# Last output projection started ahead of the last head's attention, with the attention's gated outputs transposed head by head

## The chip, the cores and the metric

One core of a Trainium2 chip runs the whole kernel. The time is the device time of one execution in microseconds, and the number compared is the median of several executions. Lower is better. TensorE (PE) has two clock levels, 2.4 and 1.2 GHz; the profile gives the granted clock as a share of the full one. The other engines here are VectorE (DVE), ScalarE (ACT) and SyncE (SP, whose queue issues the loads); GpSimd (POOL) only fills constants at the start.

## What is computed

A two-layer backbone over 256 latent tokens and 256 context tokens, width 2048. Layer 0 is gated linear attention, layer 1 differential softmax attention with 8 heads. Only the latent tokens leave layer 1. Cut to layer 1 and its end:

```python
q, k, v, g = split(h @ diff_w_in, 4)          # h: normed, modulated; 2048 -> 4 x 2048
q, k = rope(rmsnorm(q)), rope(rmsnorm(k))     # 8 heads x 2 maps x 128
p = softmax(q @ k.T * 128 ** -0.5)            # per head and map, over latent and context keys
a = p[map 0] - lam * p[map 1]
o = a @ v                                     # 8 heads x 256
o = rmsnorm(o, subln_w) * (1 - lambda_init) * silu(g)
x = x + gate[:, None] * (o @ diff_w_out)      # 2048 -> 2048
```

## The kernel before

All arithmetic is fp32. A projection is made of chunks of 512 output columns. Each takes 16 k-tiles of 128, handled as 8 pairs. To reach fp32 accuracy with fast matmuls, weights and activations are each split in a high part and a rest: three matmuls (high x low, high x high, low x high) per k-tile and tile of 128 tokens. So a pair of k-tiles costs 12 matmuls of 128x512 for the 256 latent tokens, 24 for all 512.

The weights go through a ring of four slots (`w_raw`, `w_hi`, `w_lo`). SP loads a pair's raw weights (L317) once the slot's earlier `w_raw` is split; ACT makes the high part (`split`, L433) once PE has done the pair that used the slot; DVE makes the low part (`low`, L1059); PE multiplies (`project_pair`, L749). The functions `splits` and `lows` do several pairs. Each engine works strictly in the order in which its program is written, so the order of these calls among other work is the schedule. Chunks are numbered through the kernel: layer 1 has chunks 16 to 31, two a head (keys and values, chunk c, all four token tiles; queries and gates, chunk c+1, two tiles), and the output projection 32 to 35 (OUT1 = 32).

The attention of head h-1 runs on PE between the pairs of head h's first chunk: key transposes (L986), query transposes (L993), scores (L1002, fp32), weight transposes (L1011), values (L1018, fp32). Its DVE half is `attend`: copies out of PSUM, maxima (L1499), normalised weights (L1510, L1512), copies, then the copy of the output (L1523), its squares, inverse root and gated product (L1529) into `u1`, which is a part of the big tile `u`. `keys(h)` copies chunk c's banks (L1443) and norms and rotates the keys; `queries(h)` does the same for chunk c+1 (L1469). ACT has the exponentials (L643), the SiLU of the gates with its table load (L668), and logs and exponentials for inverse roots.

Head 7 has no next head. Its attention runs alone behind chunk 31. Then four gate rows are made: DVE writes a diagonal matrix of 512 gate values (`diagonal`, L1350), PE multiplies it by ones (`gate_rows`, L960), DVE copies the broadcast row out (L1357). Then the output projection starts: `transposing(3, u1, 2)` transposes the gated output k-tile by k-tile (L777) ahead of each pair of chunk 32, DVE multiplies by the norm weight (L1143) and takes the low part (L1158), ACT takes the high part (L461). Each of the four chunks runs through all 16 k-tiles into banks 0 and 1; `result(j)` on DVE multiplies by the gate row (L1559), which frees the bank, adds the residual (L1562), and ACT issues the store (L693).

Of the kernel before, what the change touches and what calls it, by code (L numbers as in the profile page):

```python
# [73 lines left out]
ADA_USES = 7  # L74

# [20 lines left out]
def build(nc, io, out):  # L96
    with ExitStack() as ctx:
# [99 lines left out]
        u1 = u[:, 2:4, :]  # L197
# [62 lines left out]
        pv_ok = sem("pv_ok")  # L260
        lam_t, lam_pr_ok, lam_e, lam_ok = sem("lam_t"), sem("lam_pr_ok"), sem("lam_e"), sem("lam_ok")
        y_ok = sem("y_ok")
        y_out = sem("y_out")
# [9 lines left out]
        def _(sp):  # L273
# [133 lines left out]
            attention_head(A_HEADS - 1, one_range(w1, 0))  # L407
            for j in range(0, 3):
                load_chunk(j + OUT1, one_range(w1, j * CW), one_range(w1, (j + 1) * CW))
            load_chunk(CHUNKS - 1, one_range(w1, 3 * CW), None)  # L410
# [12 lines left out]
        def _(act):  # L423
# [215 lines left out]
            def softmax(h):  # L639

                for i in range(4):
                    act.wait_ge(max_ok, h * 4 + (i + 1))
                    act.activation(probs[:, i // 2, i % 2], bank[4 + i][:], ACT.Exp, bias=smx[:, 0, i:i + 1],  # L643
                                   scale=A_D ** -0.5, accum_out=smx[:, 1, i:i + 1]).then_inc(p_ok, 1)

            BATCH = G_HEADS + 2

            def attention_head(h, before):
# [13 lines left out]
                splits(c + 2, range(0, 2))  # L662
                if h % 2 == 0:
                    modulation_rows(STARTUP + 2 * G_HEADS + 4 + h // 2)
                splits(c + 2, range(2, 4))
# [19 lines left out]
            softmax(A_HEADS - 1)  # L685
            rsqrt(A_HEADS * 3 + BATCH, 2)
            high_parts(3, hfu, OUT1)

            def store(j):

                act.wait_ge(y_ok, j * 2 + 2)
                for t in range(2):
                    act.dma_start(out[0][t * P:(t + 1) * P, bass.ds(j * CW, CW)], yrow[:, t]).then_inc(y_out, 16)  # L693

            for j in range(1, 4):
                splits(j + OUT1, range(4))
                store(j - 1)
                splits(j + OUT1, range(4, 8))
            store(3)
            act.wait_ge(y_out, 4 * 2 * 16)  # L700
# [3 lines left out]
        def _(pe):  # L704
# [250 lines left out]
            def gate_rows(first, batches):  # L955
                for n in range(first, first + batches):
                    pe.wait_ge(diag_ok, n + 1)
                    if n >= first + 2:
                        pe.wait_ge(gate_ok, n - 1)
                    pe.matmul(bank[5 + n % 2][:], ones[:], diag4[n % 2].rearrange("p a b -> p (a b)"),  # L960
                              start=True, stop=True).then_inc(gate_t, 1)

# [19 lines left out]
            def key_transposes(h):  # L982
                pe.wait_ge(k_ok, h + 1)
                for m in range(2):
# [36 lines left out]

            def attention_head(h, before=None, behind=None):
# [4 lines left out]
                project(c + 1, frees(h, 1), True, tiles=2)  # L1027
# [6 lines left out]
            for step in (key_transposes, query_transposes, attention_scores, weight_transposes, attention_outputs):  # L1034
                step(A_HEADS - 1)
            pe.wait_ge(u_ok, NT * G_HEADS + 2 * A_HEADS)
            gate_rows(8, 4)
            pe.wait_ge(gate_ok, 12)

            project(OUT1, lambda t: OUT1, True, tiles=2, before=transposing(3, u1, 2))  # L1040
            for c in range(OUT1 + 1, CHUNKS):
                project(c, lambda t: c, True, tiles=2)
# [3 lines left out]
        def _(dve):  # L1046
# [391 lines left out]

            def keys(h):
                c = h * 2 + DIFF  # L1440
                for t in range(NT):
# [18 lines left out]

            def queries(h):
                c = h * 2 + (DIFF + 1)
                lows(c + 1, range(0, 2))
# [18 lines left out]
            def attend(h):  # L1482

                c = h * 2 + (DIFF + 2)
                if c < OUT1:
                    low(c, 4)
# [4 lines left out]
                if c < OUT1:  # L1491
                    low(c, 5)
                dve.wait_ge(qt_t, h + 1)
                dve.tensor_copy(qT.rearrange("p m n -> p (m n)"), bank[6][:]).then_inc(qT_ok, 1)
                if c < OUT1:
                    low(c, 6)
# [6 lines left out]
                for t in range(2):  # L1503
                    s0, s1 = smx[:, 2, 2 * t:2 * t + 1], smx[:, 2, 2 * t + 1:2 * t + 2]
                    dve.wait_ge(p_ok, h * 4 + (2 * t + 2))
                    st.step(dve.reciprocal(smx[:, 2, 2 * t:2 * t + 2], smx[:, 1, 2 * t:2 * t + 2]))
                    st.wait()
                    st.step(dve.tensor_tensor(s1, s1, lam[:, 3:4], ALU.mult))
                    st.wait()
                    st.step(dve.tensor_scalar(probs[:, t, 1], probs[:, t, 1], s1, None, ALU.mult))  # L1510
                    st.wait()
                    dve.scalar_tensor_tensor(probs[:, t, 0], probs[:, t, 0], s0, probs[:, t, 1], ALU.mult,  # L1512
                                             ALU.subtract).then_inc(a_ok, 1)
                if c < OUT1:
                    low(c, 7)
                    lows(c + 1, range(0, 2))
# [3 lines left out]
                if c < OUT1:  # L1520
                    low(c + 1, 2)
# [28 lines left out]
            def result(j, first):  # L1550
# [13 lines left out]
                if j < 3:  # L1564
                    low(j + OUT1 + 1, 3)
# [48 lines left out]
```

## Time and profile before

| | us |
|---|---|
| median of 3 runs | 1812.04 (1810.16 to 1813.54) |
| profiled execution, its own time | 1809.72 |
| its span, first to last instruction | 1807.9 |
| mean granted clock of TensorE | 0.975 |
| PE, DVE, ACT busy | 1702.6, 908.8, 557.0 |

In the rows of a time line the columns are start and duration in us, engine, line, operation, output and inputs, shapes and how many instructions were merged, and in brackets the idle time ahead of it with the instruction that ended it. A matmul's duration is modelled and longer than its distance to the next one: matmuls recorded at 0.39 us follow each other every 0.227 us.

### The profile page before, as it was taken

To read this page: it belongs to the slowest core of one execution; us is meant where nothing else is said; L and a number is where in the kernel's file an instruction comes from. 1 tells how busy PE (TensorE), PEld (TensorE's weight loads), DVE (VectorE), ACT (ScalarE), POOL (GpSimd) and SP (SyncE) were. 2 spreads that over 40 slices of the span, in tenths; PEclk is the share of its full clock that TensorE was granted. 3 is DMA by queue.
4 is the path that set the end of the run, shared out by engine and by line. 5 is a ranking of instruction groups with operands and counts; after the bars stand their busy time and mean duration, and the time that the engine had idled before them with its cause. 6 is when DMAs were issued, how large, how long until landed. Compare 5 with 4: busy or idle time off the path is not lost.

```text
span 1807.9 us, 19679 instructions
## 1 busy us (share of the span) xinstructions
PE 1702.6 (94%) x8012; PEld 1280.8 (71%) x8012; DVE 908.8 (50%) x1534; ACT 557.0 (31%) x813; POOL 2.2 (0%) x9
## 2 busy tenths in 40 slices
PE   4888999999999999989999799999999999998698
PEld 1455786678678777857777587877787787776476
DVE  2326443545264425536333557575564756557564
ACT  3213332333233313333222323242332323233232
POOL 0000000000000000000000000000000000000000
PEclk9889999999999999989999899999999999999899
DMA  8993434442443255225555326244433524423063
GB/s 314 320 332 116 164 102 153 167 163 84 140 163 106 71 175 173 72 70 164 174 191 182 105 77 232 83 139 147 147 126 117 188 80 131 160 94 121 20 197 118
DMA packets 181502, 265.54 MB, mean 147 GB/s; under 512 B 11978, under 2 KB 95876, under 8 KB 180868
## 3 DMA queue, kind: packets, MB, share of 16 engines
q1 hardware_dynamic: 175680, 256.16, 42.9%
q10 hardware_dynamic: 5732, 8.13, 1.5%
q8 instruction: 63, 1.03, 0.2%
q14 instruction: 27, 0.22, 0.0%
HBM read 262.14 MB, written 2.10 MB: 146 GB/s over the span
## 4 chain that ended last, share of the span: by engine, by line
PE 88%; DVE 7%; ACT 2%; DMA 2%; issue 1%; ACTq 1%; SPq 0%; DVEq 0%
PE bank L749 70%; PE bank L716 5%; PE bank L931 2%; PE bank L880 2%; PE bank L1018 2%; PE bank L1002 2%; PE bank L724 1%; DVE w_lo L1059 1%; DVE work L1135 1%; PE bank L876 1%; PE bank L777 1%; ACT w_hi L433 1%; DMA sel_sb<-in_sel 1%; DVE work L1379 1%; DVE u L1382 0%
## 5 line engine op out<-in xcount | busy, mean ns | idle before, releaser
L749 PE MATMUL bank<-w_lo,acts_hi 128*128 128x512 f32 x1664 | 669.1, 402 | 14.9 <-DVE acts_lo L1158 7.1
L749 PE MATMUL bank<-w_hi,acts_lo 128*128 128x512 f32 x1664 | 651.1, 391 | 0.0
L749 PE MATMUL bank<-w_hi,acts_hi 128*128 128x512 f32 x1664 | 651.0, 391 | 0.0
L1059 DVE TENSOR_TENSOR w_lo<-w_raw,w_hi 128x1024 fp32r<-128x1024 f32 x288 | 351.2, 1222 | 489.9 <-ACT w_hi L433 489.6
L433 ACT ACTIVATE w_hi<-w_raw 128x1024 fp32r<-128x1024 f32 x288 | 303.6, 1057 | 880.0 <-PE bank L749 866.9
L749 PEld LDWEIGHTS bank<-w_lo,acts_hi 128*128 128x128 f32 x1664 | 314.1, 189 | 129.9 <-issue 39.7
L749 PEld LDWEIGHTS bank<-w_hi,acts_lo 128*128 128x128 f32 x1664 | 313.8, 189 | 67.2
L749 PEld LDWEIGHTS bank<-w_hi,acts_hi 128*128 128x128 f32 x1664 | 314.5, 189 | 62.4 <-issue 1.7
L749 PE MATMUL bank<-acts_hi,w_lo 128*128 128x512 f32 x256 | 107.6, 420 | 15.6 <-DVE acts_lo L1180 15.6
L749 PE MATMUL bank<-acts_hi,w_hi 128*128 128x512 f32 x256 | 103.4, 404 | 0.0
L749 PE MATMUL bank<-acts_lo,w_hi 128*128 128x512 f32 x256 | 103.1, 403 | 0.0
L716 PE MATMUL bank<-ada_w,silu_p 128*32 128x512 f32 x624 | 86.8, 632 | 4.3 <-DMA ada_w<-in_ada_w 4.3
L749 PEld LDWEIGHTS bank<-acts_hi,w_lo 128*128 128x128 f32 x256 | 50.3, 196 | 43.3 <-DVE acts_lo L1180 19.2
L1114 DVE TENSOR_TENSOR mod<-bank,cols 128x8 f32<-128x8 f32 x24 | 3.9, 163 | 112.1 <-PE bank L724 112.1
L749 PEld LDWEIGHTS bank<-acts_lo,w_hi 128*128 128x128 f32 x256 | 50.2, 196 | 11.4
L749 PEld LDWEIGHTS bank<-acts_hi,w_hi 128*128 128x128 f32 x256 | 50.3, 197 | 10.7 <-issue 0.7
L931 PE MATMUL bank<-work 128*128 128x512 f32 x96 | 42.0, 593 | 0.0
L880 PEld LDWEIGHTS bank<-work 128*64 128x64 f32 (+1 forms) x512 | 37.8, 150 | 4.9
L880 PE MATMUL bank<-work 128*64 128x64 f32 (+2 forms) x512 | 40.7, 256 | 0.0
L461 ACT ACTIVATE acts_hi<-work 128x512 fp32r<-128x512 f32 (+1 forms) x48 | 25.6, 553 | 43.6 <-DVE work L1143 30.8
L1158 DVE TENSOR_TENSOR acts_lo<-work,acts_hi 128x512 fp32r<-128x512 f32 (+1 forms) x48 | 28.6, 595 | 18.5 <-ACT acts_hi L461 18.2
L716 PEld LDWEIGHTS bank<-ada_w,silu_p 128*32 128x32 f32 x624 | 12.9, 110 | 33.6 <-issue 25.2
(163 smaller groups left out, 1185.1 us busy)
## 6 DMA issues: line engine op xcount, KB each, us to landing
ada_w<-in_ada_w SPq DMA_DIRECT2D x78, 1024.0 KB, 7.6
w_raw<-in_diff_w_in SPq DMA_DIRECT2D x256, 256.0 KB, 3.0
w_raw<-in_gla_w_in SPq DMA_DIRECT2D x192, 256.0 KB, 3.1
u<-in_ada_w SPq DMA_DIRECT2D x16, 1024.0 KB, 9.2
w_raw<-in_gla_w_out SPq DMA_DIRECT2D x64, 256.0 KB, 3.5
w_raw<-in_diff_w_out SPq DMA_DIRECT2D x64, 256.0 KB, 3.6
u<-in_x SPq DMA_DIRECT2D x2, 1024.0 KB, 6.1
u<-in_ctx SPq DMA_DIRECT2D x2, 1024.0 KB, 10.7
```

The lines of the kernel that those rows point to most:

```text
L433: act.activation(w_hi[:, p % RING], raw[:, p % RING], ACT.Copy).then_inc(w_hi_ok, 1)
L461: act.activation(hi[:, k, 0:n * P], src[:, k % 2, 0:n * P], ACT.Copy).then_inc(hi_ok, 1)
L716: last = pe.matmul(b[32 * j:32 * j + 32, :], silu_p[:, 4 * q + j, :], quad_slot[slot][:, j, :], start=(q == 0), stop=(q == 3), skip_group_ ...
L724: last = pe.matmul(b[:, 2 * n:2 * n + 2], ada_rows[:, n * P:(n + 1) * P], sel[:], start=(n == 0), stop=True, skip_group_check=True)
L749: last = pe.matmul(bank[t][:], a, b, start=(k == 0 and i == 0), stop=(k == NK - 1 and i == 2))
L777: last = pe.transpose(bank[4 + k % 3][:, t * P:(t + 1) * P], src[:, t, k * P:(k + 1) * P], ident[:])
L880: return pe.matmul(out_, k_part, q_part, start=start, stop=True, skip_group_check=True)
L931: last = pe.matmul(bank[4 + t % 3][:], at[:, b, col:col + P], v_sb[:, kt, :], start=(i == 0), stop=(i == len(READ[t]) - 1))
L1002: pe.matmul(bank[4 + i][:], qT[:, m, t * P:(t + 1) * P], kT[:, m, :], start=True, stop=True)\
L1018: last = pe.matmul(bank[6][:, t * A_DV:(t + 1) * A_DV], aT[:, kt, t * P:(t + 1) * P], kv[:, kt, A_DV:CW], start=(kt == 0), stop=(kt == NT ...
L1059: dve.tensor_tensor(w_lo[:, p % RING], raw[:, p % RING], w_hi[:, p % RING].bitcast(F32), ALU.subtract)\
L1158: dve.tensor_tensor(lo[:, k, 0:width], buf[:, k % 2, 0:width], hi[:, k, 0:width].bitcast(F32), ALU.subtract).then_inc(acts_ok, 1)
```

## The change

The gated output of each head is kept where the attention output was (`o1`), and PE transposes it in the next head's second chunk, behind its pair 1, into bank 5. DVE multiplies it by the norm weight into `uT1`, a full transposed tile in the place of `u1`. In head 7's second chunk PE also makes the four gate rows, and DVE their diagonals and copies, in the two parts of `ada_w`. ACT and DVE make the high and low parts of k-tiles 0 to 13 behind the splits of the first output pairs.

The output projection becomes 32 output pairs in a new order: chunk 0's pairs 0 to 6, chunk 1's pairs 0 to 6, then pair 7 of chunk 0 and of chunk 1, then chunks 2 and 3 as before. Chunks 0 and 2 use banks 0 and 1, chunks 1 and 3 banks 2 and 3. Head 7's attention steps stand behind output pairs 1, 3, 4, 9, 10 and 13. The loads follow the new order; stores 0 and 1 are issued one behind the other.

```diff
+def out1_pair(s):
+    if s < 14:
+        return s // 7, s % 7
+    if s < 16:
+        return s - 14, 7
+    return s // 8, s % 8
+OUT1_DONE = (15, 16, 24, 32)
...
-        u1 = u[:, 2:4, :]
+        uT1 = u[:, 2:4, :].rearrange("p t (k n) -> p (t k) n", n=2 * P)
+        gate1 = ada_w[:, 0].rearrange("p j n -> p (j n)")
+        diag1 = [ada_w[:, 1, i].rearrange("p (a b) -> p a b", b=P) for i in range(2)]
...
# ACT
+            def high_out1(p):
+                for k in (2 * p, 2 * p + 1):
+                    if p < 7:
+                        act.wait_ge(u1T_ok, p + 1)
+                        act.wait_ge(pair_done, (OUT1 - 1) * PAIRS + (p + 1 + RING))
+                    else:
+                        act.wait_ge(u1T_ok, A_HEADS)
+                    act.activation(hi[:, k, 0:2 * P], uT1[:, k], ACT.Copy).then_inc(hi_ok, 1)
...
+                if h == A_HEADS - 1:
+                    for p in range(4):
+                        split(c + 2, p)
+                        high_out1(p)
...
-            softmax(A_HEADS - 1)
+            for p in range(4, 7):
+                split(OUT1, p)
+                high_out1(p)
+            splits(OUT1, range(7, 8))
+            splits(OUT1 + 1, range(0, 1))
+            softmax(A_HEADS - 1, range(0, 2))
+            splits(OUT1 + 1, range(1, 2))
+            softmax(A_HEADS - 1, range(2, 4))
+            splits(OUT1 + 1, range(2, 7))
             rsqrt(A_HEADS * 3 + BATCH, 2)
-            high_parts(3, hfu, OUT1)
+            high_out1(7)
+            splits(OUT1 + 1, range(7, 8))
...
+            splits(OUT1 + 2, range(4))
+            store(0)
+            store(1)
+            splits(OUT1 + 2, range(4, 8))
...
# PE
+            def output_transposes(h):
+                pe.wait_ge(u_ok, NT * G_HEADS + 2 * h + 2)
+                for j in range(2):
+                    for t in range(2):
+                        last = pe.transpose(bank[5][:, (2 * j + t) * P:(2 * j + t + 1) * P],
+                                            o1[:, t, j * P:(j + 1) * P], ident[:])
+                last.then_inc(ut_t, 1)
...
+                def second(p):
+                    if h > 0 and p == 1:
+                        output_transposes(h - 1)
+                    if h == A_HEADS - 1 and p in (1, 2, 6, 7):
+                        gate_rows({1: 8, 2: 9, 6: 10, 7: 11}[p])
+                project(c + 1, frees(h, 1), True, tiles=2, after=second)
...
+            def output_pair(s):
+                j, kp = out1_pair(s)
+                c, p = OUT1 + s // PAIRS, s % PAIRS
+                pe.wait_ge(w_split, c * PAIRS + (p + 1 + RING))
+                for e in range(2):
+                    k, wh, wl = 2 * kp + e, w_hi[:, p % RING, e], w_lo[:, p % RING, e]
+                    if j < 2:
+                        pe.wait_ge(acts_ok, 3 * NK + k + 1 if j == 0 else 4 * NK if kp == 7 else 3 * NK + 14)
+                    for t in range(2):
+                        b = 2 * (j % 2) + t
...
+            behind_last = {1: key_transposes, 3: query_transposes_last, 4: attention_scores, 9: weight_transposes,
+                           10: attention_outputs, 13: output_transposes}
+            for s in range(4 * PAIRS):
+                output_pair(s)
+                if s in behind_last:
+                    behind_last[s](A_HEADS - 1)
...
# DVE, keys(7) and queries(h)
+                if h == A_HEADS - 1:
+                    dve.wait_ge(ada_taken, STARTUP + BACKGROUND)
+                    for i in range(2):
+                        gate_diagonal(8 + i, i)
...
+                if h > 0:
+                    outputs_out(h - 1)
+                if h == A_HEADS - 1:
+                    for i in range(2):
+                        gate_out(8 + i, i)
+                        gate_diagonal(10 + i, i + 2)
+                    for p in range(2):
+                        low(c + 1, p)
+                        low_out1(p)
...
+                if h == A_HEADS - 1:
+                    low_out1(2)
+                    gate_out(10, 2)
...
# DVE, behind queries(7)
+            gate_out(11, 3)
+            low_out1(3)
+            low(OUT1, 4)
+            low_out1(4)
+            keys_out(last_head)
+            low(OUT1, 5)
+            low_out1(5)
+            low(OUT1, 6)
+            low_out1(6)
+            queries_out(last_head)
+            low(OUT1, 7)
+            low(OUT1 + 1, 0)
+            maxima(last_head)
+            low(OUT1 + 1, 1)
+            weights(last_head, 0)
+            low(OUT1 + 1, 2)
+            weights(last_head, 1)
+            lows(OUT1 + 1, range(3, 5))
+            weights_out(last_head)
+            low(OUT1 + 1, 5)
+            gated(last_head)
+            low(OUT1 + 1, 6)
+            outputs_out(last_head)
+            low_out1(7)
+            low(OUT1 + 1, 7)
...
+            lows(OUT1 + 2, range(0, 3))
+            result(0)
+            low(OUT1 + 2, 3)
+            result(1)
+            lows(OUT1 + 2, range(4, 8))
+            lows(OUT1 + 3, range(0, 3))
+            result(2)
+            lows(OUT1 + 3, range(3, 8))
+            result(3)
```

`gate_diagonal` and `gate_out` are one DVE product of 128x512 and one DVE copy of 128x512; `outputs_out` is two DVE products of 128x256 out of bank 5; `low_out1(p)` two DVE subtractions of 128x256. `keys_out`, `queries_out`, `maxima`, `weights`, `weights_out` and `gated` are the parts of the former `attend`, unchanged but for where `gated` writes.

## Rows read from the trace of the kernel before

**Rows 1.** The page: engines' busy time, the w_lo group, the weight loads.

```profile
PE 1702.6 (94%) x8012; PEld 1280.8 (71%) x8012; DVE 908.8 (50%) x1534; ACT 557.0 (31%) x813; POOL 2.2 (0%) x9
L1059 DVE TENSOR_TENSOR w_lo<-w_raw,w_hi 128x1024 fp32r<-128x1024 f32 x288 | 351.2, 1222 | 489.9 <-ACT w_hi L433 489.6
w_raw<-in_diff_w_out SPq DMA_DIRECT2D x64, 256.0 KB, 3.6
```

**Rows 2.** Busy time by stretch: length, PE, PEld, DVE, ACT, POOL, clock, DMA share, GB/s.

```profile
1639.30:1661.20 21.90, 21.90 (x97) 18.09 (x97) 18.04 (x26) 8.69 (x10) 0.00 (x0) 1.00 0.50 161
1661.20:1706.20 45.00, 22.42 (x61) 12.18 (x60) 27.74 (x60) 9.34 (x19) 0.00 (x0) 0.73 0.08 27
1706.20:1733.00 26.80, 26.04 (x120) 20.41 (x121) 19.79 (x36) 12.26 (x22) 0.00 (x0) 1.00 0.32 105
1733.00:1756.10 23.10, 22.35 (x97) 17.89 (x97) 12.32 (x13) 8.51 (x9) 0.00 (x0) 1.00 0.70 219
```

**Rows 3.** The chain of waits, last head's attention: start us, us, what.

```profile
1672.92 3.64 PE bank L1002 x4
...
1684.52 6.38 PE bank L1018 x16
```

**Rows 4.** Time line of PE beside projections: transposes, scores, values.

```profile
1598.42 0.60 PE L993 MATMUL bank<-ident_sb,work 128*128 128x128 f32 x4
1598.77 0.48 PE L749 MATMUL bank<-w_lo,acts_hi 128*128 128x512 f32 x1
...
1604.33 3.59 PE L1002 MATMUL bank<-work 128*128 128x512 f32 x8
...
1630.43 3.61 PE L1018 MATMUL bank<-work 128*128 128x256 f32 x16
```

**Rows 5.** Time line: the copies ahead of chunk 31, its first matmul, two diagonals.

```profile
1638.52 2.48 DVE L1443 COPY work<-bank 128x512 f32<-128x512 f32 x4
1639.35 0.47 PE L749 MATMUL bank<-w_lo,acts_hi 128*128 128x512 f32 x1
...
1695.47 1.29 DVE L1350 TENSOR_TENSOR work<-ident_sb,mod 128x512 f32<-128x512 f32 x2
```

**Rows 6.** Time line of DVE: w_lo in a queue, the last head's query chain.

```profile
1651.62 2.35 DVE L1059 TENSOR_TENSOR w_lo<-w_raw,w_hi 128x1024 fp32r<-128x1024 f32 x2
1653.89 0.68 DVE L1427 TENSOR_TENSOR work<-work 128x512 f32<-128x512 f32 x1
...
1661.01 1.28 DVE L1469 COPY work<-bank 128x512 f32<-128x512 f32 x2
...
1670.29 0.68 DVE L1427 TENSOR_TENSOR work<-work 128x512 f32<-128x512 f32 x1
```

**Rows 7.** Time line: from a transposed tile to its high and low part.

```profile
1703.83 0.88 DVE L1143 TENSOR_SCALAR work<-bank,cols 128x256 f32<-128x256 f32 x2 [0.53 <-PE bank L777]
1704.35 0.81 ACT L461 ACTIVATE acts_hi<-work 128x256 fp32r<-128x256 f32 x2 [10.61 <-DVE work L1143]
...
1704.80 0.42 DVE L1158 TENSOR_TENSOR acts_lo<-work,acts_hi 128x256 fp32r<-128x256 f32 x1
```

**Rows 8.** Time line of PE: first matmuls of a later output chunk, the very last.

```profile
1756.08 0.47 PE L749 MATMUL bank<-w_lo,acts_hi 128*128 128x512 f32 x1 [0.44 <-DVE work L1559]
...
1757.31 0.51 PE L749 MATMUL bank<-w_lo,acts_hi 128*128 128x512 f32 x1 [0.30 <-DVE work L1559]
...
1801.56 0.39 PE L749 MATMUL bank<-w_hi,acts_lo 128*128 128x512 f32 x1
```

**Rows 9.** A matmul after a short wait; a stretch (columns as in rows 2).

```profile
1092.52 0.47 PE L749 MATMUL bank<-w_lo,acts_hi 128*128 128x512 f32 x1 [1.78 <-DVE work L1443]
...
1692.00:1694.00 2.00, 0.00 (x0) 0.00 (x0) 1.39 (x5) 0.41 (x2) 0.00 (x0) 0.83 0.00 0
```

**Rows 10.** Time line of PE: the first pair of chunk 12, layer 0's output projection.

```profile
803.72 0.80 PE L749 MATMUL bank<-w_lo,acts_hi 128*128 128x512 f32 x1 [2.78 <-DVE acts_lo L1158]
...
809.01 0.52 PE L749 MATMUL bank<-w_lo,acts_hi 128*128 128x512 f32 x1
```

More of the change, by code:

```diff
@@ L637, in _, with softmax @@
             high_parts(2, hf, DIFF)
-            def softmax(h):
-                for i in range(4):
+            def softmax(h, parts=range(4)):
+                for i in parts:
                     act.wait_ge(max_ok, h * 4 + (i + 1))
@@ L952, in _ @@
                 gla_head(h)
[L955 to L961, printed above, removed]
             def block_gates(j):
@@ L1020, in attention_outputs, with gate_rows @@
                 last.then_inc(pv_ok, 1)
+            def output_transposes(h):
[5 more added lines that the diff above has]
+                last.then_inc(ut_t, 1)
+            def gate_rows(n):
+                pe.wait_ge(diag_ok, n + 1)
+                if n >= 10:
+                    pe.wait_ge(gate_ok, n - 1)
+                pe.matmul(bank[6 + n % 2][:], ones[:], diag1[n % 2].rearrange("p a b -> p (a b)"),
+                          start=True, stop=True).then_inc(gate_t, 1)
             def attention_head(h, before=None, behind=None):
@@ L1033, in _, with query_transposes_last @@
                                           5: weight_transposes, 6: attention_outputs})
[L1034 to L1042, printed above, removed]
+            def query_transposes_last(h):
+                pe.wait_ge(gate_ok, 12)
+                query_transposes(h)
+            def output_pair(s):
[8 more added lines that the diff above has]
+                        b = 2 * (j % 2) + t
+                        if k == 0:
+                            pe.wait_ge(freed[b], (OUT1 if b < 2 else DIFF + A_HEADS) + j // 2)
+                        x = slice(t * P, (t + 1) * P)
+                        for i, (a, w) in enumerate(((hi[:, k, x], wl), (hi[:, k, x], wh), (lo[:, k, x], wh))):
+                            last = pe.matmul(bank[b][:], a, w, start=(k == 0 and i == 0), stop=(k == NK - 1 and i == 2))
+                        if k == NK - 1 and t == 0:
+                            last.then_inc(acc_ok, 1)
+                last.then_inc(pair_done, 1)
+            behind_last = {1: key_transposes, 3: query_transposes_last, 4: attention_scores, 9: weight_transposes,
[4 more added lines that the diff above has]
+                    behind_last[s](A_HEADS - 1)
         @block.vector
@@ L1519, in attend, with gated @@
                     dve.tensor_copy(flat(aT[:, 2 * b:2 * b + 2]), bank[4 + b][:]).then_inc(aT_ok, 1)
-                if c < OUT1:
-                    low(c + 1, 2)
+            def gated(h):
                 dve.wait_ge(pv_ok, h + 1)
@@ L1528, in attend @@
                 for t in range(2):
-                    dve.scalar_tensor_tensor(u1[:, t, bass.ds(h * A_DV, A_DV)], o1[:, t], stat[:, 2, t:t + 1],
-                                             silu_ag[:, t], ALU.mult, ALU.mult).then_inc(u_ok, 1)
+                    dve.scalar_tensor_tensor(o1[:, t], o1[:, t], stat[:, 2, t:t + 1], silu_ag[:, t], ALU.mult, ALU.mult)\
+                        .then_inc(u_ok, 1)
+            def attend(h):
+                c = h * 2 + (DIFF + 2)
+                low(c, 4)
+                keys_out(h)
+                low(c, 5)
+                queries_out(h)
+                low(c, 6)
+                maxima(h)
+                for t in range(2):
+                    weights(h, t)
+                low(c, 7)
+                lows(c + 1, range(0, 2))
+                weights_out(h)
+                low(c + 1, 2)
+                gated(h)
             lows(DIFF + 1, range(0, 3))
@@ L1567, in _ @@
-            result(0, True)
-            for j in range(1, 4):
-                result(j, False)
+            last_head = A_HEADS - 1
+            gate_out(11, 3)
[12 more added lines that the diff above has]
+            low(OUT1 + 1, 1)
```

134 lines of the change are left out of this document (71 added, 63 removed).

## Prediction

> **What bounds the kernel now.** I read the page first: PE is busy 1702.6 of 1807.9 us [rows 1], so only time in which PE stands still, or runs at its lower clock, can be won. The table by stages says where that is [rows 2]. Projection chunk 31 (1639.3 to 1661.2) is PE from end to end at clock 1.00. Then come 45.0 us with 22.42 us of PE at a mean clock of 0.73: the last head's attention, four gate rows and the first transposes of the output, with no projection to fill the waits. The first output chunk takes 26.8 us (transposes and waits between its matmuls), the later ones about 23.1. The chain of waits inside the 45 us goes back and forth between DVE and PE, and PE's share runs at the low clock: the four scores matmuls are on it for 3.64 us though only part of them shows, and the 16 value matmuls for 6.38 us [rows 3], against 3.3 us for the same 16 beside the projections [rows 4]. So the end is set by PE's work after 1639.35 plus PE's waits, and the largest wait is the one gap.
>
> **The unit prices.** One pair of k-tiles with two token tiles is 12 matmuls; 96 matmuls of chunk 31 take 21.8 us, so a pair costs 2.72 us. Beside projections a group of 4 transposes costs 0.45 us (from 1598.42 to 1598.77 and 0.1 more before the next matmul runs evenly), 8 cost 0.9, the 4 scores matmuls 3.4 and the 16 value matmuls 3.4 (recorded at 3.59 and 3.61, which overlap their neighbours by 0.2) [rows 4]. A gate row is one fp32 matmul of 128x512 like a score: 0.9 us each with its switch. On DVE, two w_lo take 2.27 us (1651.62 to the next start at 1653.89), so 1.14 each when queued [rows 6]; a 128x512 copy or diagonal in a queue is 0.62 to 0.65 [rows 5, 6]; a low part of 128x256 is recorded at 0.42 [rows 7] and costs 0.35 to 0.4 in a queue.
>
> **PE's work after 1639.35, part by part.** The moved work isn't less, it only lies elsewhere. Chunk 31 and the 32 output pairs: 40 x 2.72 = 108.8. Beside them: two groups of output transposes (heads 6 and 7) 0.9, gate rows 3.6, key transposes 0.9, query transposes 0.45, scores 3.4, weight transposes 0.85, values 3.4: together 13.5. Heads 0 to 5 are transposed earlier, inside chunks that run without a gap, so 6 x 0.45 = 2.7 us are added there in full; the DVE copies behind them (2 x 0.4 us a head) fall into DVE's waits for ACT before its w_lo (489.9 us before 288 of them, 1.7 each [rows 1]), and cost nothing while these last. Sum without waits: 125.0. In the trace the same stretch lasts to 1801.56 + 0.23 = 1801.8 [rows 8], 162.4 us.
>
> **The waits that I expect, by walking the queues.** (a) Two gate diagonals stand on DVE ahead of the copies that free banks 0 and 1 for chunk 31. Today the copy starts at 1638.52 and PE at 1639.35, just when chunk 30 ends [rows 5], so there is no slack: 1.2 us. (b) After chunk 31 and gate row 11 (0.9) PE needs bank 0, which DVE copies only behind the low parts of output pairs 0 to 2 and one gate copy. DVE reaches it about 1.0 us after chunk 31's end, frees it at 1.7: 0.8 us. Two pairs, key transposes and a pair take PE to 10.8 us after chunk 31. (c) The queries' chain (copies to the rotated result, 1661.01 to 1670.97, so 8.7 us behind the copies' end [rows 6]) ends at 10.9; behind it the last gate copy (0.62) and a low part (0.4) let PE start pair 3 at about 11.9: 1.0 us. Pair 3, query transposes, pair 4 end near 17.8. (d) DVE has in its queue, before the copy of the transposed queries: 3 w_lo (3.4), 7 low parts (2.6), key copies (1.3), and that copy (0.65): 8.0 us from 11.9, so the scores start at 19.8: 2.0 us. (e) From there five pairs cover maxima and softmax: DVE needs 3.2 (maxima), 3.2 (weights) and four w_lo (4.6), with ACT waiting once for a pair; my walk has the weights ready 4 us before PE has done pair 9, the transposed weights 2 us before pair 10 ends, and the gated output 3.5 us before pair 13 ends. So none. (f) Behind the last output transposes there is nothing to fill: DVE's two copies, ACT's high part, DVE's low part, 1.9 us in all (0.48 + 0.4 + 0.45 + 0.42 and latencies, after 1703.83, 1704.35 and 1704.80 [rows 7]). (g) At the switch to the third chunk DVE has three w_lo ahead of the multiply that frees bank 0: 0.8, and 0.5 more for bank 1, much like today's 0.44 and 0.30 as shown plus gaps that the modelled ends hide, 1.1 in all [rows 8]. The third-to-fourth switch uses the other banks: none. Sum 1.2 + 0.8 + 1.0 + 2.0 + 1.9 + 1.3 = 8.2 us.
>
> The ring of four weight slots gives 8.2 us from the release of a slot to its use, against 1.22 us for DVE's part of a split and less for ACT's, and weight loads (3.6 us to landing [rows 1]) are asked for one ring turn ahead; SP's queue holds only those. The stores of result chunks 0 and 1 are issued on ACT one behind the other, ahead of the split of pair 4 of the third chunk; it waits to about 1732 and is used at 1737. ACT's high parts (2 x 0.41 a pair) fit in its waits. The tail behind PE's last matmul stays: two multiplies, two adds, the store.
>
> **The sum.** 125.0 + 8.2 + 0.2 for further switches = 133.4 us instead of 162.4: 29.0 less. The profiled execution took 1809.72 us at a span of 1807.9; the median of the runs is 1812.04. I take 29 us from the median: 1783.0 us.
>
> **Unknown costs and bounds.** No row shows a short copy behind transposes of head h-1 competing in chunk c+1; it lies between 0 (hidden, as the w_lo of [rows 6] are) and 7 x 0.8 = 5.6 us on PE; I take 0, as those waits are seen everywhere. Nor does one show output pairs with 6 waits in 55 us. If DVE is 20% quicker through the walk than I book it, the waits shrink by 2 to 3 us (no lower: PE's 125.0 are fixed). If it is 20% slower, (b), (c), (d) grow by about 4 us.
>
> **Weighed against the skill: the clock.** The trace shows what waits do to PE's clock. After 1.78 us of waiting the matmul at 1092.52 took 0.47 us, a full-speed one [rows 9]. Idle from 1690.9 on (the end of the value matmuls [rows 3]), the clock fell to its lower level some 2.4 us later: 0.83 over 1692 to 1694 is 1.00 for 1.3 us and 0.50 for the rest [rows 9]. At 803.72, after 2.78 us of waiting, twelve matmuls ran 5.3 us instead of 2.7 and only then came back to 2.4 GHz [rows 10]. My longest waits, (d) and (f), are 2.0 and 1.9, between these. The Trainium skill, "TensorE: Matmul & The Clock Gate", section "A second HAM failure mode: psum-queue depth-cycling", says that many short idles between matmul groups make the clock swing between its two levels; by that rule this order, with six short waits, could lose some of its gain. The trace agrees for idles of 2.4 us and more and not for 1.8.
>
> **Rivals.** (1) The clock falls to 1.2 GHz once or twice behind (d) or (f). For it: the 2.4 us row. Against it: the 1.78 us row, and the dense matmuls on both sides. Price 2.6 us each from [rows 10], up to 3.4 if it hits the scores or values (which double): 1786 to 1790. (2) DVE becomes the bound of the last head: from the last quarter of chunk 31 to the weights it hardly rests, and as its queue is strict, lateness shows in (b), (c), (d) and then in the ring. Twice the waits (b) to (f), 7 more: 1788 to 1794. Against it: PE's five pairs of cover. (3) The walk books too much waiting: 1777 to 1780. (4) Slower than before: the clock, once down in (c) or (d), doesn't come back through the mixed stretch of pairs, transposes and fp32 matmuls. PE work at 1.2 GHz takes twice its time, so 29 us of full-speed work must be run at the low level, that is 58 us of the time, before the change loses; the whole mixed stretch and a chunk at it: 1816. For it: the last head's 16 value matmuls took 6.38 us, low for their whole length [rows 3]; against it, one dense pair restored 2.4 GHz at 809 [rows 10]. (5) The change doesn't overlap as it says, PE in order waiting for the last head's chain ahead of the output pairs: about 1808. The walk finds PE's waits (the freed bank, one low part, the transposed queries) far short of that.
>
> **How the numbers follow.** Forecast 1783.0, own range 1780 to 1786: 60%. Rival 1: 18%. Rival 2: 11%. Rival 3: 6%. Rival 4: 2%. Rival 5: 3%. The range reaches from the edge of rival 3 over rival 1 and half of rival 2: 1779.5 to 1791. A measurement of this kernel tells about 0.2% (3.6 us) from no change; faster by more has all of 1, 2, 3 and the forecast and half of 5: 0.96; within 0.2%: 0.02; slower: 0.02.
>
> **What would show it.** The first output pair should start about 1.7 us after chunk 31's last matmul, and scores, value matmuls and both transposes stand between output pairs. Chunk 31 should start 1.2 us late behind a COPY at DVE. PE's waits in the stretch should sum to 8 us with the two longest before the scores and before the first k-tile of pair 7; clock 1.00 throughout; PE's last matmul 29 us earlier. Wrong would be: waits before w_split (the ring starved), a clock under 1.00 between chunk 31 and the end, or gaps in heads 1 to 6 beyond 0.45 us each.

## The result and the profile after

The changed kernel takes 1781.46 us (1781.14 to 1782.85), beside 1811.1 us for the one before in the same comparison: ratio 0.9838, interval 0.9821 to 0.9855, 29.6 us less. The forecast was 1783.0. The profiled execution took 1782.85 us at a span of 1780.9, 27.0 us under the span before. It is the slowest of its four; 1.6 us of it are a fall of the clock that is shown below. The same kernel was run and profiled once more later, 1782.86 us at a span of 1781.0 ("changed again" below).

Busy time by stretch in the changed kernel (columns as in [rows 2]):

```profile
1642.60:1664.50 21.90, 20.84 (x90) 16.46 (x90) 19.89 (x32) 8.84 (x13) 0.00 (x0) 1.00 0.37 120
1664.50:1687.70 23.20, 20.92 (x92) 15.70 (x90) 20.71 (x42) 13.96 (x22) 0.00 (x0) 1.00 0.41 134
1687.70:1723.00 35.30, 33.32 (x145) 26.37 (x146) 21.89 (x40) 10.94 (x19) 0.00 (x0) 1.00 0.42 136
...
1731.00:1774.70 43.70, 43.40 (x191) 35.40 (x189) 22.61 (x25) 12.82 (x13) 0.00 (x0) 1.00 0.53 159
```

The 45 us with half of PE idle at a mean clock of 0.73 [rows 2] are gone. From chunk 31 to the last output pair PE is busy for at least nine tenths of each stretch, and DVE for about as much of the first two.

Who PE waited for from 1640 to 1775, changed kernel (total us, times, longest):

```profile
PE bank L1121 <- DVE acts_lo L1578: 2.7, 2, 2.0
PE bank L1048 <- DVE work L1622: 1.2, 1, 1.2
PE bank L802 <- DVE work L1548: 1.1, 1, 1.1
PE bank L1121 <- DVE work L1720: 0.7, 2, 0.4
PE bank L1121 <- DVE work L1602: 0.3, 1, 0.3
```

L802 is the projection, L1121 the output pairs, L1048 the scores. These are the waits (a) L1548, (b) L1602, (c) and (f) L1578, (d) L1622 and (g) L1720 of the prediction, and no other. In this stretch PE did not wait for a split pair of weights (w_split). The idle shown is less than the loss, because a matmul's recorded end is modelled. By distance to the next start, less 0.23 us for a matmul that simply follows, they are:

| wait | booked | measured |
|---|---|---|
| (a) ahead of chunk 31 | 1.2 | 1.2 |
| (b) first output pair | 0.8 | 0.5 |
| (c) pair 3 | 1.0 | 0.9 |
| (d) scores | 2.0 | 1.4 |
| (f) behind the last output transposes | 1.9 | 2.1 |
| (g) switch to the third chunk | 1.3 | 1.1 |
| sum | 8.2 | 7.2 |

The time line of the changed kernel at some of these places, PE and DVE (columns as before):

```profile
1569.17 0.60 PE L1072 MATMUL bank<-ident_sb,work 128*128 128x128 f32 x4
1569.52 0.48 PE L802 MATMUL bank<-w_lo,acts_hi 128*128 128x512 f32 x1
...
1641.78 1.29 DVE L1532 TENSOR_TENSOR ada_w<-ident_sb,mod 128x512 f32<-128x512 f32 x2
1642.98 2.48 DVE L1548 COPY work<-bank 128x512 f32<-128x512 f32 x4
...
1686.98 0.68 DVE L1622 COPY work<-bank 128x512 f32<-128x512 f32 x1
...
1722.74 0.47 PE L1121 MATMUL bank<-w_lo,acts_hi 128*128 128x512 f32 x1 [1.97 <-DVE acts_lo L1578]
```

The first two rows answer [rows 4]: a head's output transposes take 0.35 us to the next matmul and nothing waits for them. The diagonals at 1641.78 push the bank copies behind the end of chunk 30 (1642.6); in [rows 5] the copies start before that end.

The one thing that the table of waits lacks is the clock. Changed kernel, profiled execution, then the later execution of the same kernel:

```profile
1721.00:1723.00 2.00, 0.26 (x1) 0.29 (x2) 1.45 (x4) 1.28 (x3) 0.00 (x0) 1.00 0.07 26
1723.00:1725.00 2.00, 2.00 (x7) 1.54 (x7) 1.58 (x2) 2.00 (x3) 0.00 (x0) 0.57 0.00 0
1725.00:1727.00 2.00, 2.00 (x7) 1.58 (x6) 1.92 (x2) 0.28 (x1) 0.00 (x0) 0.58 0.47 151
```

```profile
1722.00:1724.00 2.00, 0.40 (x4) 0.16 (x2) 1.08 (x3) 0.65 (x3) 0.00 (x0) 1.00 0.28 102
1724.00:1726.00 2.00, 1.63 (x7) 1.40 (x8) 1.51 (x3) 2.00 (x4) 0.00 (x0) 1.00 0.00 0
```

In the first, PE falls to 1.2 GHz behind wait (f) for about 3.4 us; the pair takes 4.4 us instead of 2.8. In the second the same wait of 1.97 us leaves the clock alone. This was expected of the second execution before it ran: the fall may stay away or move, and 1.6 us in this stretch would show it (191.2 against 189.6 us in the table below). As a whole it was no faster than the first, 1782.86 against 1782.85, because its clock fell earlier in the kernel, behind a wait near 1090 us.

### The profile page after: what moved, and what is told of

Its sections match the earlier page's. It is cut to its first block, busy times and chain, and to the rows that moved or that the text cites. A ratio compares the mean times of both kernels' runs of the same rounds, so it can differ in the third digit from the quotient of the medians.

```text
span 1780.9 us, 19693 instructions
## 1 busy us (share of the span) xinstructions
PE 1691.0 (95%) x8012; PEld 1276.5 (72%) x8012; DVE 906.5 (51%) x1534; ACT 555.5 (31%) x813; POOL 2.2 (0%) x9
## 4 chain that ended last, share of the span: by engine, by line
PE 88%; DVE 7%; DMA 2%; ACT 2%; issue 1%; ACTq 1%; SPq 0%; DVEq 0%
PE bank L802 67%; PE bank L769 5%; PE bank L1121 4%; PE bank L984 2%; PE bank L933 2%; PE bank L1048 2%; PE bank L1064 2%; PE bank L777 1%; DVE w_lo L1148 1%; DVE work L1224 1%; PE bank L929 1%; DMA sel_sb<-in_sel 1%; DVE work L1468 1%; PE bank L830 1%; DVE u L1471 1%
## 5 line engine op out<-in xcount | busy, mean ns | idle before, releaser
L802 PE MATMUL bank<-w_lo,acts_hi 128*128 128x512 f32 x1536 | 619.5, 403 | 13.3 <-DVE acts_lo L1247 6.1
L802 PE MATMUL bank<-w_hi,acts_lo 128*128 128x512 f32 x1536 | 600.8, 391 | 0.0
L802 PE MATMUL bank<-w_hi,acts_hi 128*128 128x512 f32 x1536 | 600.3, 391 | 0.0
L802 PEld LDWEIGHTS bank<-w_lo,acts_hi 128*128 128x128 f32 x1536 | 289.6, 189 | 121.2 <-issue 39.3
L802 PEld LDWEIGHTS bank<-w_hi,acts_lo 128*128 128x128 f32 x1536 | 289.5, 188 | 62.6
L802 PEld LDWEIGHTS bank<-w_hi,acts_hi 128*128 128x128 f32 x1536 | 290.2, 189 | 58.3 <-issue 2.4
L802 PE MATMUL bank<-acts_hi,w_lo 128*128 128x512 f32 x256 | 107.0, 418 | 15.6 <-DVE acts_lo L1269 15.6
L802 PE MATMUL bank<-acts_hi,w_hi 128*128 128x512 f32 x256 | 102.6, 401 | 0.0
L802 PE MATMUL bank<-acts_lo,w_hi 128*128 128x512 f32 x256 | 102.5, 400 | 0.0
L802 PEld LDWEIGHTS bank<-acts_hi,w_lo 128*128 128x128 f32 x256 | 49.9, 195 | 43.2 <-DVE acts_lo L1269 19.2
L802 PEld LDWEIGHTS bank<-acts_lo,w_hi 128*128 128x128 f32 x256 | 49.8, 195 | 11.2
L802 PEld LDWEIGHTS bank<-acts_hi,w_hi 128*128 128x128 f32 x256 | 50.1, 196 | 10.5 <-issue 0.7
L1121 PE MATMUL bank<-w_lo,acts_hi 128*128 128x512 f32 x128 | 51.9, 405 | 3.8 <-DVE acts_lo L1578 2.7
L1121 PE MATMUL bank<-w_hi,acts_lo 128*128 128x512 f32 x128 | 50.6, 396 | 0.0
L1121 PE MATMUL bank<-w_hi,acts_hi 128*128 128x512 f32 x128 | 50.4, 394 | 0.0
```

What stands on the lines that cost most here:

```text
L802: last = pe.matmul(bank[t][:], a, b, start=(k == 0 and i == 0), stop=(k == NK - 1 and i == 2))
L1121: last = pe.matmul(bank[b][:], a, w, start=(k == 0 and i == 0), stop=(k == NK - 1 and i == 2))
```

## The experiments

All experiments start from the changed kernel. Several effects are smaller than what executions of one kernel differ by ahead of the last head: the first matmul of chunk 30 came at 1589.73 in one and at 1591.36 in the other execution of the changed kernel. Those 1.6 us come from that earlier fall (rows in the last section). So beside the times I compare the stretch from that matmul to the end of the span ("last stretch"):

| kernel | time, us | last stretch, us |
|---|---|---|
| before | 1811.1 | 221.4 |
| changed | 1781.5 | 191.2 with the fall of the clock, 189.6 without (changed again) |
| alone | 1803.1 | 212.9 |
| alone_warm | 1799.8 | 207.9 |
| one_chunk | 1790.1 | 197.7 |
| scores_early | 1785.5 | 195.2 |
| diag_late | 1778.6 | 190.2 (with a fall) |
| out_early | 1780.5 | 187.4 |
| all_three | 1775.5 | 184.9 |
| five | 1772.0 | 182.1 |
| dve_keys2 | 1784.2 | 192.6 |
| dve_weights2 | 1781.2 | 191.1 (with a fall) |

Those of alone, alone_warm, one_chunk, all_three and five are medians of four; the rest of the experiments ran once each, so for them the last stretch carries the argument, and not the time.

**Is it the cover?** The last head's attention put back in front of the output pairs:

```diff
-            behind_last = {1: key_transposes, 3: query_transposes_last, 4: attention_scores, 9: weight_transposes,
-                           10: attention_outputs, 13: output_transposes}
+            behind_last = {}
+            for step in (key_transposes, query_transposes_last, attention_scores, weight_transposes,
+                         attention_outputs, output_transposes):
+                step(A_HEADS - 1)
```

with DVE's and ACT's parts of it ahead of the splits of pair 4 and later.

> The changed kernel, but the last head's attention and its output transposes stand ahead of all output pairs on PE, and its DVE and ACT parts ahead of the weights' splits from pair 4 on; transposing head by head, early gate rows, pair order and banks stay. Theory (the gain is the cover that output pairs give to the last head's attention): the attention's chain is bare again, PE's first output pair starts about 19 us later against the work left, 1800 us, and the clock falls again in the scores and value matmuls. Rival (the gain comes from early transposes, early gate rows and the banks; the order of attention and pairs matters little): below 1787 us.

It took 1803.1 us (0.9951 of before, 0.9935 to 0.9968). PE's four longest waits from 1640 us on:

```profile
PE bank L1034 <- DVE ada_w L1535: 9.1, 1, 9.1
PE bank L1067 <- DVE work L1654: 4.6, 1, 4.6
PE bank L1052 <- DVE work L1638: 4.1, 1, 4.1
PE bank L1043 <- DVE work L1619: 1.4, 1, 1.4
```

The last stretch is 23.3 us longer than the changed kernel's at full clock. So the cover is most of the gain; what is left of it, 7.8 us by the medians, is early transposes, early gate rows and the second pair of banks together, which no run separates. The forecast of 19 was 4 us short; how much low clock it held is not on record.

**What part of that is the clock?** The same kernel with PE kept at work in the waits:

```diff
+            def spin(n):
+                pe.wait_ge(freed[2], DIFF + A_HEADS)
+                for _ in range(n):
+                    pe.matmul(bank[2][:, 0:P], ones[:], ident[:], start=True, stop=True)
...
+            key_transposes(last_h)
+            spin(36)
+            query_transposes_last(last_h)
```

> As the previous kernel, with fp32 matmuls of 128x128 on constant tiles (into a bank that is overwritten later) put into PE's waits between the attention steps: 36, 4, 17, 4, 20 and 7 of them. Theory: what the overlap gains is mostly the waits themselves; keeping PE active keeps 2.4 GHz and gives back only the low-clock part, 1.9 us at the scores, 0.5 at the weight transposes and 3.0 at the values: about 5.5 us under the previous kernel, 1795. Rival (the low clock was the main loss of the gap): 10 us or more under it.

The clock stayed at 1.00 until the end of the work, and the last stretch is 4.9 us shorter (medians: 3.3), close to the 5.5 expected. The clock is worth more than that: the last group of fillers stands where alone has no wait. There the first output pair starts 0.76 us behind the start of the output transposes (1705.28 to 1706.04), and here 1.97 us (1699.62 to 1701.59). With these 1.2 us, about 6 of the 23.3 us that the cover is worth are clock and 17 are the waits themselves.

Time line of PE in alone, the weight transposes and the values, and then in alone_warm, the scores (as the values beside projections [rows 4], the scores are at full speed there; in alone the values run as long as in [rows 3]):

```profile
1692.08 1.10 PE L1052 MATMUL bank<-ident_sb,work 128*128 128x128 f32 x8 [4.12 <-DVE work L1638]
1694.12 6.55 PE L1059 MATMUL bank<-work 128*128 128x256 f32 x16 [0.94 <-DVE work L1644]
```

```profile
1680.93 3.70 PE L1043 MATMUL bank<-work 128*128 128x512 f32 x8 [0.92 <-DVE work L1634]
```

**Is one chunk enough cover?** Order by chunks, with the weight transposes behind pair 5, values and output transposes behind pair 6:

```diff
-    if s < 14:
-        return s // 7, s % 7
-    if s < 16:
-        return s - 14, 7
     return s // 8, s % 8
```

> The changed kernel with only chunk 0 of the output projection as cover: all 8 pairs of chunk 0, then chunk 1, and so on; weight transposes behind pair 5, values and output transposes behind pair 6; result 0 is taken early. Theory: 2 instead of 9 pairs lie between the scores and the output transposes, so PE waits 2.3 us for the weights, 4.5 for the gated output and 2.0 for its high and low parts, while the switch between chunks 1 and 2 no longer waits: about 5 to 7 us slower than the changed kernel, 1787. Rival (one chunk covers enough, the second chunk and its banks are not needed): within 1.5 us of the changed kernel.

1790.1 us (0.9882, 0.9867 to 0.9897), against 1787 expected, and 8.1 us more in the last stretch. PE's waits:

```profile
PE bank L1066 <- DVE work L1651: 4.6, 1, 4.6
PE bank L1115 <- DVE acts_lo L1572: 2.7, 2, 2.0
PE bank L1051 <- DVE work L1635: 2.1, 1, 2.1
PE bank L1042 <- DVE work L1616: 1.2, 1, 1.2
```

The wait for the gated output (4.6, L1651) and for the weights (2.1, L1635) are the two that I had worked out, and the switch (g) is gone as expected. The last 2 us or so, which the expectation did not have, are clock: it was low from 1710 to about 1717. So the second column chunk is worth 8 of the 29 us.

**The clock by itself.** Scores ahead of output pair 4 instead of behind it, which makes wait (d) 4.0 us:

```diff
-            behind_last = {1: key_transposes, 3: query_transposes_last, 4: attention_scores, 9: weight_transposes,
+            behind_last = {1: key_transposes, 3: lambda h: (query_transposes_last(h), attention_scores(h)), 9: weight_transposes,
```

> The changed kernel with the last head's scores right behind the query transposes, ahead of output pair 4. It doubles wait (d): PE idles 4.1 us instead of 1.4 ahead of the scores. Theory (clock): after so long an idle the scores start at or soon fall to 1.2 GHz; the wait costs 2.7 us, the clock 1.6 to 3.4 more: 1786 to 1788. Rival: the clock holds at 1.00 through the scores and only the 2.7 us show, 1784. Beside that, the weights come later, since maxima stand behind a split that waits for pair 4; four pairs of slack should hide it.

Time line of PE and busy time by stretch, same kernel:

```profile
1686.35 6.67 PE L1048 MATMUL bank<-work 128*128 128x512 f32 x8 [4.01 <-DVE work L1622]
```

```profile
1684.00:1686.00 2.00, 0.00 (x0) 0.00 (x0) 2.00 (x4) 0.00 (x0) 0.00 (x0) 0.88 0.62 189
1686.00:1688.00 2.00, 1.65 (x2) 0.84 (x3) 1.42 (x2) 0.00 (x0) 0.00 (x0) 0.50 0.85 278
```

The clock fell before the scores began and held low through all of them: 6.67 us instead of 3.7, so 3.0 us for the clock on top of 2.7 for the wait. The last stretch is 5.6 us longer than the changed kernel's at full clock, which is both; nothing else came of it. The time, 1785.5, lies just under the 1786 to 1788 expected. The wait of 1.97 us at (f) was there too, without a fall.

**The waits one by one.** Diagonals behind the copies of the keys:

```diff
-                if h == A_HEADS - 1:
-                    dve.wait_ge(ada_taken, STARTUP + BACKGROUND)
-                    for i in range(2):
-                        gate_diagonal(8 + i, i)
                 for t in range(NT):
                     complete(h * 4 + 3 * DIFF, c, t)
                     dve.tensor_copy(kv[:, t], bank[t][:]).then_inc(freed[t], 1)
+                if h == A_HEADS - 1:
+                    for i in range(2):
+                        gate_diagonal(8 + i, i)
```

(the wait stays where it was).

> The changed kernel with only the two gate diagonals moved behind the copies of the last head's keys. Theory: the 1.06 us wait of PE ahead of chunk 31 goes, and stays gone, since everything behind it moves with PE: last matmul 1.1 us earlier, about 1780.3. Rival (the next wait takes it up, because DVE reaches the query copies no earlier): wait (b) grows from 0.5 to 1.6 us and the time stays.

Wait (a) was gone and all the others kept their size (1.3 at the scores, 2.0 at (f), the clock falling behind it as in the changed kernel's profiled execution). The last stretch is 1.0 us shorter than that one's: of the 1.2 us measured at (a), 1.0 came back, and (b) did not take it up. The time, 1778.6, is 1.7 us under the 1780.3 expected; chunk 30 started at 1586.56 already, and that is not the edit's.

Output transposes one pair earlier:

```diff
-                           10: attention_outputs, 13: output_transposes}
+                           10: attention_outputs, 12: output_transposes}
```

> The changed kernel with only the last output transposes moved from behind pair 13 to behind pair 12. Theory: the gated output is ready at 1716.6, pair 12 ends at 1717.4, so PE does not wait for it; pair 13 covers the 1.9 us of copies and parts, so wait (f) goes, and with no idle PE the clock stays at 1.00 there: 2.0 + 1.6 = 3.6 us, 1777.9. Rival (the fall of the clock has nothing to do with that wait): the clock still falls near 1723, 2.0 us.

Wait (f) was gone, the clock stayed at 1.00 up to the tail. The last stretch is 2.2 us shorter than the changed kernel's at full clock and 3.8 shorter than that with the fall, against 2.0 and 3.6. The time, 1780.5, missed the 1777.9 expected: this execution had the fall behind the wait near 1090 us, as changed again had it.

These two with two more, the gate copy 10 behind the query copies and `queries_out` ahead of `low(OUT1, 6)`:

```diff
+            queries_out(last_head)
             low(OUT1, 6)
             low_out1(6)
-            queries_out(last_head)
```

> The changed kernel with its waits (a), (b), (d) and (f) attacked by order alone: the two gate diagonals behind the copies of the last head's keys, the third gate copy behind the query copies, the copy of the transposed queries one pair earlier on DVE, the output transposes behind pair 12 instead of 13. Theory (the remaining waits are set by what stands ahead in DVE's queue): 1.2 + 0.5 + 1.4 + 2.0 us of waits go, and with (f) the fall of the clock at 1723 that cost 1.6: 5 to 6.7 us faster, 1775 to 1776.5. Rival (the waits are in a chain, and one removed comes back at the next): 2 us or less.

1775.5 us (0.9801, 0.9785 to 0.9817), 6.3 us less in the last stretch than the profiled execution of the changed kernel and 4.7 less than the one at full clock. Of PE's waits only two lines are left:

```profile
PE bank L1121 <- DVE acts_lo L1579: 1.3, 1, 1.3
PE bank L1121 <- DVE work L1722: 0.7, 2, 0.4
```

The total lies in the expected 1775 to 1776.5. The first line is (c), which grew from 0.9 to 1.4 us by start distances: PE comes earlier, the queries' chain does not. So a part of what (b) gave, 0.5 us, moved on to the next wait, as the rival said; the rest stayed gained.

Wait (c) and (g) on top: the fourth gate copy and the low part of pair 3 in DVE's idle time ahead of the inverse roots, and result 0 behind two splits instead of three:

```diff
                 squares(q_t, q_raw, 4)
-                inverse_rms(h * 3 + (BATCH + 2), 4, A_D)
+                if h < A_HEADS - 1:
+                    inverse_rms(h * 3 + (BATCH + 2), 4, A_D)
+                else:
+                    dve.tensor_scalar(stat[:, 1, 0:4], stat[:, 0, 0:4], 1.0 / A_D, EPS, ALU.mult, ALU.add)\
+                        .then_inc(mean_ok, 1)
+                    gate_out(11, 3)
+                    low_out1(3)
+                    dve.wait_ge(rs_ok, h * 3 + (BATCH + 2))
+                    newton(4)
...
-            lows(OUT1 + 2, range(0, 3))
+            lows(OUT1 + 2, range(0, 2))
             result(0)
-            low(OUT1 + 2, 3)
+            lows(OUT1 + 2, range(2, 4))
             result(1)
```

> The kernel with the four order edits, and two more: in the last head's queries the fourth gate copy and the low part of output pair 3 stand in DVE's wait for the inverse roots (2.2 us idle), and result 0 is taken between the low parts of the third chunk's pairs 1 and 2 instead of behind three of them. Theory (waits are set by DVE's order): wait (c), 1.45 us in that kernel, and the two waits of (g), 1.06 us, go: 2.5 us less, 1773.0. Rival (by now PE's own work bounds, or the waits move on to the scores): 1 us or less.

1772.0 us (0.9776, 0.9759 to 0.9792), and another 2.8 us less in the last stretch, for 2.5 expected. PE has no wait left:

```profile
1641.00:1667.00 26.00, 26.00 (x110) 20.02 (x110) 25.07 (x42) 11.44 (x17) 0.00 (x0) 1.00 0.43 143
1667.00:1720.00 53.00, 53.00 (x240) 42.67 (x239) 42.33 (x77) 25.58 (x41) 0.00 (x0) 1.00 0.44 142
```

DVE's wait ahead of the inverse roots, 2.2 us in the changed kernel, now holds two pieces of work (time line of DVE):

```profile
1669.06 0.69 DVE L1538 COPY ada_w<-bank 128x512 f32<-128x512 f32 x1
1669.66 0.75 DVE L1579 TENSOR_TENSOR acts_lo<-u,acts_hi 128x256 fp32r<-128x256 f32 x2
1671.49 0.16 DVE L1158 TENSOR_TENSOR stat<-stat 128x4 f32<-128x4 f32 x1 [1.08 <-ACT stat L469]
```

**Where does DVE's lateness count?** Three copies in a row put into its queue at two places, all else as in the changed kernel:

```diff
+            for _ in range(3):
+                st.step(dve.tensor_copy(d2m[:], d1m[:]))
+                st.wait()
             keys_out(last_head)
```

> The changed kernel with three DVE copies of 128x512 between unused tiles, one waiting for the other (about 0.7 us each, 2.1 in all), ahead of the copies of the last head's transposed keys. Theory (DVE's queue sets wait (d)): PE's wait before the scores grows from 1.4 to 3.5 us and the rest follows, 2.1 us slower, and the longer idle makes the fall of the clock likely (1.6 to 3 us more). Rival (DVE has slack there): the wait stays at 1.4.

```profile
1682.17 1.34 DVE L1690 COPY d2m<-d1m 128x512 f32<-128x512 f32 x3
1683.54 1.29 DVE L1618 COPY work<-bank 128x512 f32<-128x512 f32 x2
```

The three copies took 1.37 us, not 2.1: I had priced a copy out of SBUF by the rows of copies out of PSUM. The wait at (d) grew from 1.4 to 2.8 us, by just that, and the clock fell in the scores, which were recorded at 5.4 us instead of 3.7. Last stretch 3.0 us longer.

The same ahead of `weights_out`:

> The same three DVE copies, but ahead of the copies of the last head's transposed weights. Theory (five pairs and more cover this part, the prediction booked 2 us of slack for the transposed weights): no new wait of PE before the value matmuls, time as the changed kernel within 0.5 us beside its clock. Rival (DVE is the bound of the whole last head): 2.1 us slower there too.

PE had no new wait; the last stretch equals that of the changed kernel with its fall of the clock (191.1 and 191.2), and a fall behind (f) was there as well.

## Why the prediction was right

The forecast of 1783.0 stands 1.5 us above the median, and the mechanism is the one that it walked through. By the traces the sum of 133.4 us fits within 0.1: 132.1 measured behind chunk 30, 3.0 for the transposes ahead of it, less 1.6 for the fall of the clock, are 133.5. That this is so close is partly luck, because three errors cancel: the waits were booked 1.0 too high, the switches 0.8 and the transposes 0.3 too low. And the fall of the clock was not in the sum: in the profiled execution PE's last matmul came 27.1 us earlier (1774.46 for 1801.56), not 29, and a clock under 1.00 behind chunk 31, which the prediction names as a sign of being wrong, did occur there.

**PE's fixed work.** Booked 125.0 us behind the start of chunk 31, of which 2.7 for heads 0 to 5 ahead of it. The measured stretch from the end of chunk 30 (1642.6) to PE's last matmul (1774.7) is 132.1 us; less 7.2 of waits and 1.6 of clock it is 123.3, against 122.3 + 0.2 booked. The 0.8 left lie in small amounts at the switches between kinds of work; the first matmul behind each wait, for one, takes 0.08 us longer. (The prediction's 16 value matmuls are 16 records of 8 fp32 matmuls; the price of the group stands.)

**The waits.** All six came where they were booked, no other came, and the sum was 1 us high. The term most off is (d), 2.0 for 1.4. Its largest part is the price of a low part of 128x256: seven were booked at 2.6 us, and two of them take 0.67, so seven 2.35. The copies were 0.15 us cheaper as well, and PE's pairs and transposes ahead of (d) 0.15 dearer. In (b), 0.3 high, six low parts stand in the queue at the same price.

**The cover in (e).** The walk had 4 us of slack for the weights, 2 for the transposed weights, 3.5 for the gated output. In the changed kernel the weights are ready at 1700.9 and pair 9 ends at 1705.1, the copies end at 1706.8 and pair 10 at 1708.7, the gated output is ready at 1716.7 and pair 13 ends at 1720.2: 4.2, 1.9 and 3.5. The experiment with 1.4 us more of DVE work there cost nothing; that fits the 1.9, but doesn't measure it.

**Heads 1 to 6.** Booked at 0.45 us each and nothing for DVE's copies. Chunk 30 starts 3.2 us later than before in one execution (1586.50 against 1589.73) and 4.9 in another, of which 1.6 is the fall of the clock behind the wait near 1090 us. From the first matmul behind that wait, which stands ahead of all six groups of transposes (1092.52 in [rows 9], 1092.78 after), to chunk 30 it is 493.98 us before and 496.95 after: 3.0 us, 0.5 a group, against 0.45 booked. One head apart, the first matmuls at 1505.70 and 1586.50 are 80.8 us from each other before, and 81.3 (1508.44 to 1589.73) after: 0.5 us for the group of transposes and nothing for DVE's copies.

**Rival 1, the clock,** had 18%. Its mechanism did take place, beside the forecast and not instead of it: the wait of 1.97 us at (f) stands unchanged in six profiled executions, and the clock fell behind it in three (changed, diag_late, dve_weights2) and not in three (changed again, scores_early, dve_keys2). It cost 1.6 us, for 2.6 booked. The price and the reading of [rows 10] were wrong: the low clock there was not brought by the wait of 2.78 us. It had begun by 800 (granted clock 0.51 from 799 to 801), in a longer idle ahead of four transposes (before, time line of PE):

```profile
799.83 1.11 PE L777 MATMUL bank<-ident_sb,u 128*128 128x128 f32 x4 [4.26 <-DVE work L1143]
```

At (f) the clock fell only 0.5 us into the pair and came back after 3.4 us. The rule that the prediction takes from the Trainium skill, "TensorE: Matmul & The Clock Gate", section "A second HAM failure mode: psum-queue depth-cycling", is borne out here: short idles between groups of matmuls can make the clock swing. How many of the four timed executions had the fall isn't known; the trace of one shows it. That the median landed under the forecast is within the noise of the comparison: the executions of before span 5 us.

**Rival 2** (DVE as the bound) is answered by the pair of DVE experiments: ahead of the scores 1.4 us of DVE were 1.4 us of PE, behind them 1.4 us cost nothing. Rival 3 was right in its direction, by 1 us of waits, and not in its size. Rivals 4 and 5 did not occur; alone is close to what 5 would have looked like, and it took 22 us more than the changed kernel, where 5 had 25 over the forecast.

## What to carry to other kernels

When a serial chain between engines ends a phase, count the work of the bounding engine that can stand between its steps, and check each step's slack against what is queued ahead of it on the other engines; one column chunk as cover (with 2 pairs between the scores and the output transposes) was worth 15 of the 23 us here, a second one 8. The waits that remain are then a matter of order on the helping engine: six reorderings without any new work gave 7.5 us more by the last stretch at full clock, 9.5 by the medians. An idle of 2 us on PE costs more than 2 us on average here, because in about half of the cases (counted below) the clock falls behind it, at a price of about 1.5 us.

## What the runs showed of the hardware

I had not expected the same idle of 1.97 us, with the same work around it, to be followed by half clock in three executions and by full clock in three. The length of the idle doesn't decide it alone. A wait for DVE's bank copies, ahead of layer 1's second chunk, stands in all thirteen traces, with 1.50 to 2.51 us. Changed kernel, then changed again (time line of PE):

```profile
1092.78 0.47 PE L802 MATMUL bank<-w_lo,acts_hi 128*128 128x512 f32 x1 [2.51 <-DVE work L1548]
```

```profile
1092.87 0.76 PE L802 MATMUL bank<-w_lo,acts_hi 128*128 128x512 f32 x1 [2.09 <-DVE work L1548]
```

The second matmul is at the low clock. With 1.50 to 1.79 us (before, scores_early, dve_keys2, dve_weights2) the clock never fell. From 1.90 us on it fell in four of nine: with 2.09 (changed again), 2.10 (out_early), 2.28 (diag_late) and 2.31 (one_chunk), and not with 1.90, 2.06, 2.19, 2.21 and 2.51. The four with a fall need 417.1 to 417.2 us from there to the first matmul of chunk 28, the other eight traces with the change 415.7 to 415.8: 1.4 to 1.5 us. With 4.01 us ahead of the scores (scores_early, one execution) the clock fell before the work came back. fp32 matmuls of 128x128 on constant tiles in the waits of the bare attention kept the clock at 1.00 throughout (alone_warm). And three DVE copies of 128x512 between SBUF tiles, each waiting for the one before, take 1.37 us, where two out of PSUM take 1.2.
